# Latent rows of the expert stage: taken one by one instead of in pairs

## What is computed

```
def block(args):
    xb, ib, gb = args
    act = jnp.einsum("td,thkd->thk", xb, u_tab[ib])
    return jnp.einsum("thk,thkd->td", jax.nn.gelu(act) * gb, v_tab[ib])
```

## Time and profile before

| | us |
|---|---|
| median of three runs (lowest, highest) | 2408.23 (2406.45, 2408.54) |
| the profiled execution | 2407.21 |
| its span from first to last record | 2405.4 |
| busy: TensorE, VectorE | 1656.4 (69%), 1567.2 (65%) |
| busy: GpSimd, ScalarE | 977.5 (41%), 343.4 (14%) |
| mean rate of the DMA engines over the span | 403 GB/s |

### The profile page before, as it was taken

The page is one execution under the profiler, slowest core; times in us unless marked ns, Lnnn a source line. Parts: engine busy times, 40 slices in busy tenths (PEclk is TensorE's granted clock), DMA queues, the critical chain, the costliest instruction groups (busy, mean ns, idle before and its releaser), DMA issues.

```text
span 2405.4 us, 21904 instructions
## 1 busy us (share of the span) xinstructions
PE 1656.4 (69%) x6740; PEld 666.9 (28%) x6740; DVE 1567.2 (65%) x4471; ACT 343.4 (14%) x973; POOL 977.5 (41%) x1028
## 2 busy tenths in 40 slices
PE   5899858896567667776656796888555556555654
PEld 2445533481123121223211263365111101110110
DVE  0339986778854665654687789587975555755555
ACT  1322143110010122200001124311000000000000
POOL 0004537556532333332333546755733333333332
PEclk8999878996688886787878897999677777787787
DMA  9989999999999999999999999998999999999997
GB/s 369 404 343 360 409 419 408 413 413 382 416 422 423 403 421 419 380 424 422 397 422 419 396 412 371 409 414 352 395 422 421 421 422 416 422 418 422 409 421 291
DMA packets 164327, 969.47 MB, mean 403 GB/s; under 512 B 18122, under 2 KB 20554, under 8 KB 88690
## 3 DMA queue, kind: packets, MB, share of 16 engines
q0 software_dynamic: 147456, 805.37, 82.2%
q1 hardware_dynamic: 16754, 162.70, 16.4%
HBM read 964.85 MB, written 3.15 MB: 402 GB/s over the span
## 4 chain that ended last, share of the span: by engine, by line
DMA 50%; PE 19%; DVE 19%; issue 8%; ACT 3%; POOL 1%; SPq 0%; POOLq 0%; DVEq 0%; ACTq 0%
DMA work<-peer_uv_in,vidx 21%; DMA ring<-peer_uv_in,vidx 18%; DMA wring<-peer_uv_in,vidx 4%; DVE ring L2084 4%; PE acc L1187 3%; PE psum L857 3%; PE psum L884 2%; DMA ring<-peer_uv_in,idx 2%; PE psum L1133 2%; DMA lent_line<-peer_uv_in,vidx 2%; PE acc L1209 2%; DVE work L1614 2%; DVE work L1609 1%; PE acc L783 1%; POOL ring L766 1%
## 5 line engine op out<-in xcount | busy, mean ns | idle before, releaser
L766 POOL DMA_INDIRECT ring<-peer_uv_in,vidx x366 | 350.4, 957 | 437.8 <-PE acc L1187 144.1
L1187 PE MATMUL acc<-work,cond 128*32 128x512 f32 x884 | 299.9, 801 | 174.6 <-DVE cond L2051 174.5
L1187 PE MATMUL acc<-ring,cond 128*32 128x512 f32 x784 | 254.6, 768 | 211.0 <-DVE cond L2051 211.0
L766 POOL DMA_INDIRECT work<-peer_uv_in,vidx x258 | 247.9, 961 | 365.0 <-PE acc L1187 132.8
L2071 DVE CUSTOM_DVE_ANT_0 work<-work,h_kept 128x1024 f32<-128x1024 f32 x221 | 268.8, 1219 | 188.3 <-DMA work<-peer_uv_in,vidx 178.2
L2071 DVE CUSTOM_DVE_ANT_0 ring<-ring,h_kept 128x1024 f32<-128x1024 f32 x196 | 236.8, 1218 | 147.8 <-DMA ring<-peer_uv_in,vidx 132.0
L766 POOL DMA_INDIRECT ring<-peer_uv_in,idx x193 | 182.4, 945 | 348.9 <-DVE idx L1731 204.0
L2084 DVE CUSTOM_DVE_ANT_0 ring<-ring,h_kept 128x1024 f32<-128x1024 f32 x193 | 225.3, 1216 | 15.6 <-DMA ring<-peer_uv_in,idx 14.3
L1511 ACT ACTIVATE dots<-dots 128x2 f32<-128x2 f32 x256 | 52.0, 203 | 1043.0 <-DVE dots L2071 1042.9
L1187 PEld LDWEIGHTS acc<-work,cond 128*32 128x32 f32 x884 | 54.8, 132 | 399.9 <-DVE cond L2051 252.5
L1133 PE MATMUL psum<-work,wring 128*128 128x256 f32 (+1 forms) x896 | 163.0, 344 | 3.0 <-ACT work L1251 3.0
(11 more groups left out here) (257 smaller groups left out, 2170.8 us busy)
## 6 DMA issues: line engine op xcount, KB each, us to landing
wring<-w_in_in SPq DMA_DIRECT2D x17, 2048.0 KB, 11.6
wring<-peer_wq_in SPq DMA_DIRECT2D x14, 2048.0 KB, 10.4
wring<-mod_w_in SPq DMA_DIRECT2D x10, 2048.0 KB, 10.3
ring<-mod_w_in SPq DMA_DIRECT2D x9, 2048.0 KB, 12.5
wring<-w_out_in SPq DMA_DIRECT2D x8, 2048.0 KB, 12.5
work<-mod_w_in SPq DMA_DIRECT2D x5, 2048.0 KB, 14.7
ring<-w_in_in SPq DMA_DIRECT2D x3, 2048.0 KB, 22.8
ring<-peer_uv_in,vidx POOLq DMA_INDIRECT x366, 11.7
```

What stands on the lines that cost most here:

```text
L766: nc.gpsimd.indirect_dma_start(row(kind, k, t, r)[0], None, io["peer_both" if kind == "f" else "peer_one"], bass.IndirectOffsetOnAxis(ap=a ...
L1187: ins = mm(acc[half][lane:lane + QUAD, :], vw_duo(k, t, i)[:, j * QUAD:(j + 1) * QUAD], held[:, D + half * CHUNK:D + (half + 1) * CHUNK], ...
```

## The change

Three constants and the list of events change:

```
-DUO = 2
+DUO = 1
 DUOS = PICKS // DUO
-VW_DUOS = 3
-BESIDE_CHOOSING, BEHIND_CONTEXT = 25, 10
+VW_DUOS = 7
+BESIDE_CHOOSING, BEHIND_CONTEXT = 50, 20
 LENT_ROW, LEFT_ROWS = 8, 8
-BESIDE_AHEAD = 2, 1, 2, 1, 2
+BESIDE_AHEAD = 4, 2, 4, 2, 4
...
         if t < st.T:
             if i * DUO % QUAD == 0:
                 events.append(("h", st.k, t, i * DUO // QUAD))
-            events.append(("f", st.k, t, i * DUO))
+            events.append(("f", st.k, t, i))
         if n:
             events += [("m", *before), ("p", *before)]
...
         if t < st.T:
-            events += [("f", st.k, t, i * DUO + 1), ("e", st.k, t, i)]
+            events.append(("e", st.k, t, i))
     return events
```

## The result

The changed kernel takes 2422.5 us (median of 6 runs, 2418.1 to 2426.0), the kernel before 2409.1 beside it: ratio 1.0056, interval 1.0044 to 1.0069, 13.4 us slower. Forecast were 2404 us and a range up to 2415; the time lies outside. The profiled execution took 2419.6 us, 12.4 more than before's 2407.2.

The account below looks back on a forecast made before the run. Bound by DMA bytes over rate, plus stretches where gathers wait for freed rows. Terms -2.0 - 1.5 + 0.7 - 1.8 - 0.6 + 1.0 = -4.2 us gave 2403.0 profiled, 2404 us as median; range 2394 to 2415.

Parts of the forecast that it names:

- the tail is closed: Last latent stretch, 1780 to 2380 us: gathering at 419 GB/s with nothing else running, so no loss to win back.
- Added work on VectorE: 256 weighings become 512: 0.125 us more a row, 64 us beside transfers, of which 1 us was charged for backlogs.
- D: Hole at 1190 to 1200 us, after the choice's first round: row 62 freed before the spread, gain 1.8 of 3.1 us.
- VectorE fills up: Rival: VectorE saturates beside the choice of experts, 5.5 us (up to 7.3) shows as DMA idle time; 2414 us, chance 0.17.
- C: Hole at 1000 to 1010 us, end of tile 0 at twelve long matmul passes: net +0.7 us, ends -2 and +4.
- The first two chances: Chances of the outcomes against the kernel before: faster 0.41, same 0.42, with the forecast's 0.50 split half each side of 2403.4.
- In the tail this costs nothing: VectorE's added time in the last latent stretch: a row lands every 2.48 us and takes VectorE 1.43, so no cost.
- A: Hole at 800 to 830 us, behind the fifth input projection: first V sum comes sooner, gain 2.0 of 2.8 us.
- B: Hole at 970 to 980 us, behind an attention head: one row freed before the delayed GELU, gain 1.5 us, all of it.
- The ends: Last dot to addition to x in both latent steps: two of four matmuls run during the GELU, gain 0.6 us.
- EARLY: Event count that now puts 8 instead of 13 rows ahead of the next step: 0 us, nothing downstream starts earlier.
- The rival that the clock would rise: All four holes close, through fewer unfreed rows or TensorE keeping its higher clock into the blocks: 2394 us, chance 0.17.

Follow-up runs that it names:

- the waits moved away: Changed kernel with the wait for the weights' place moved from VectorE to ScalarE, 512 fewer VectorE instructions: 2417.7 us, ratio 1.0055 to the kernel before.
- the waits added: Kernel before with 1006 already satisfied waits more on VectorE, ahead of each latent row's dot: 2417.7 us, ratio 1.0046.
- the run that undid it: Changed kernel with row 127's weighing and V sum and the addition to x again ahead of the twelve long passes: 2418.4 us, ratio 1.0046.
- two runs: Changed kernel with EARLY = 48 instead of 30: 2417.6 us, ratio 1.0041; kernel before with EARLY = 18: 2410.6 us, ratio 1.0013.
- the third run: Row by row, weight and spreading in one, wait on ScalarE, EARLY = 48, a cut-off weighing and V sum laid ahead of the long passes: 2412.5 us, ratio 1.0028.
- the last three runs: Weight and spreading in one, wait on ScalarE: row by row 1.0005; with 13 rows ahead and a sum moved 1.0028; in pairs 0.9992, against the kernel before.
- the wait for pairs: Changed kernel in which TensorE holds an even row's V sum until the odd row's weights are ready: 2422.9 us, ratio 1.0071 to the kernel before.

## Why the prediction was wrong

**What bounds the kernel** held: the rate, with few places for rows. Not held: "the tail is closed". The tail was not free of loss, it had a late gather every 91 us, and I read the slice's 419 against 422 as nothing.

**Added work on VectorE** is where it failed: the step put 1.0 us on the added time and had no term for the added instructions. The size of the work was right: 512 products at 155 ns and 512 spreadings, the latter forecast at 190:

```profile
L2043 DVE TENSOR_TENSOR wv<-dots,idx x512: 148/155/227, 638.5 to 2403.0; 128x1 f32<-128x1 f32 x171
...
L2051 DVE TENSOR_TENSOR cond<-const,wv x512: 191/192/268, 638.6 to 2403.2; 128x32 f32<-128x32 f32 x171
```

and 1.44 us a row where I had 1.43. (VectorE's busy time rose by 53.8 us to 1621.0 and not by 79, in part because records overlap: in the earlier trace rows the product starts at 1009.99 and the dot ends at 1010.07.) I charged 1.0 us for it, since VectorE was busy 97.2 of 110 us beside the choice of experts. That share is an average over the choice and its gaps. The time alone costs about 6 us (10.6 against 4.5 with the same number of instructions; the error allows 2 to 11). Where it costs them is not shown. A slower backlog ahead of the choice is 0.4 of the 4.4 us at D, and in pairs half the added time left that stretch as long as before. The rival "VectorE fills up" named the mechanism, priced it at 5.5, and got 0.17. Its sum is short: 5.5 and C's 4 are 9.5 us, not the 6 that it adds to 2408. The first two chances should be 0.42 and 0.41 by its own rule.

The number of instructions was no term at all. A packet costs 0.9 us by the waits moved away (14.1 less 10.6 us for four packets, not clear of the noise between jobs) and 1.3 by the waits added (10.1 us for eight); VectorE has six more, so 5 to 8 us. "In the tail this costs nothing" is the same omission: 3.3 us.

**A** was forecast to gain 2.0; its slices went from 380, 372 and 397 to 352, 409 and 425 with 399 ahead of them: 0.3 us. **B** gained its 1.5. **C** was put at +0.7 with +4 as its upper end: 3.5 in its slices (1000 to 1020 us), 3.4 by the run that undid it. The step counted TensorE's sooner start as a gain and forgot that the V sums left out of it freed rows. **D**, forecast to gain 1.8, lost about 4: the step took the end of the choice's round as fixed, and it came 4.4 us later, by 2.0 for the lower clock of the query projection ahead, 0.7 for its later start, 1.3 for the rows that the cut now puts ahead of the round, and 0.4 for VectorE's pace. The new hole near 1290 us, 2.7, stands unexplained. **The ends**: 0.6 at most, and not seen. **EARLY**, put at 0: between 3 us (two runs) and -4 (the third run, which moved a cut too). Moves of the cuts give plus or minus 4 us that I can't sum from the trace; the 3 us that are left of row by row in the last three runs (1.0005 against 0.9992) are of that size.

Together: 5 to 8 for the number, 6 for the time, 0 to 3 for order and cuts give 11 to 17; measured 13.4 and 14.1. The terms are read from runs of this same case, so the agreement proves little. The waits for a GELU were to grow fewer; they are one fewer and longer (before: the earlier trace rows), 640 to 1340 us:

```profile
DVE wv L2043 <- ACT dots L1511: 82.9, 16, 10.6
```

The rival that the clock would rise had the sign wrong (0.78 to 0.66 in the tail), and the wait for pairs gave at most 1.5 us back there. The Trainium skill's Perfetto Trace Analysis, section Optimizing Scalar/DVE Operations, says that grouping small operations can improve throughput if the engine is saturated. Here one operation for two brought 9.6 us though VectorE was busy only 67% of the span, so the runs agree with the rule and not with its condition.

## What to carry to other kernels

Where the time is set by transfers, count the instructions of each engine, not only their time: waits included, 128 of VectorE's more cost about 1 us here, ScalarE's nothing that could be told from zero. A low busy share does not make added time free: 0.13 us a row cost some 6 us on an engine busy 67% of the span. When a place is late, split the lateness by engine before naming a cause; at D the added work was the smallest part. And before splitting an operation, look whether two that follow each other with a wait between can be one: that alone brought 9.6 of 14 us back.

## What the runs showed of the hardware

- An instruction packet of VectorE (128 instructions, 8 KB) goes with a gather 0.95 us late while the rows' queue is full; 8 KB are 1/128 of a row. Twelve packets more for ScalarE left no trace. The Trainium skill, Runtime: NRT & Kernel Launch, section Instruction fetch mechanics, has refills that are mostly hidden; ScalarE's agree, VectorE's don't. Why they differ no run here shows, nor why the eight packets cost 10.1 us in one job and at most 5.3 in the slower one.
- TensorE's granted clock depends on how its work is bunched: the same matmuls of the tail got 0.66 of full when they came row by row and 0.75 to 0.78 in pairs. 58 us less busy time there shortened the tail by 1.5 us and the whole by nothing. In a dense block that rows wait for it counts: 32 matmuls took 5.88 us at 0.66 and 3.84 at 1.00.
- In one job the kernel before took 2542 us, in the others 2407 to 2409. The loss lay up to the first addition to x (705 us in the run with waits on VectorE, 631 in the first profile) and in step 3 (471 against 401), where context rows are gathered; the other stretches were shorter than elsewhere (tails of 638 to 643 against 648). It is not shown to be the chip: the record gives the same number, 8, to this job and to a later one of 2407.0 us. In the slow job the row-by-row kernel with weight and spreading in one beat the pairs (0.9973), elsewhere it did not (1.0019).
